# Splitting the final RMSNorm over the output projection, and reordering loads around the merge loop, in a one-layer hybrid decoder kernel

## The reference, cut to what matters

```python
merged = sigmoid(gate_r) * (ret_branch @ w_ret_proj) + sigmoid(gate_s) * (sb_branch @ w_sb_proj)
h = x + merged @ w_out
r = lax.rsqrt(jnp.mean(h * h, axis=-1, keepdims=True) + EPS_RMS)
y = h * r * final_norm_gain                  # y_prompt (512 x 2048), y_sample (64 x 2048)
```

## Time and profile before

| | |
|---|---|
| three timed runs | 2132.35, 2132.97 (median), 2134.16 us |
| profiled execution, its own time | 2128.34 us |
| its span, first to last instruction | 2126.6 us |
| mean granted TensorE clock | 0.988 |
| PE, DVE, ACT, POOL busy | 97%, 70%, 45%, 6% |

### The profile page before, as it was taken

One profiled execution on the slowest core, in us unless ns is written; L12 is line 12 of the kernel. 1 busy time (PEld: TensorE's weight loads), 2 busy tenths in 40 slices (PEclk: granted clock), 3 DMA queues, 4 the chain that ended last, 5 costly groups with the idle time before them and its releaser, 6 DMA issues.

```text
span 2126.6 us, 42199 instructions
## 1 busy us (share of the span) xinstructions
PE 2067.3 (97%) x15584; PEld 1989.3 (94%) x15584; DVE 1487.0 (70%) x1915; ACT 965.1 (45%) x1345; POOL 132.7 (6%) x141
## 2 busy tenths in 40 slices
PE   7999999999999999999999999999999989988996
PEld 6999999999999999999999999999999989988996
DVE  6866766666772377778878878878787644457776
ACT  5545545445563345454454444454555521233333
POOL 0022212122200000000000000000000000000000
PEclk9999999999999999999999999999999999999998
DMA  4445554454554443334333343334436353453444
GB/s 152 126 134 145 147 146 141 137 146 139 146 159 141 140 134 114 111 91 120 110 112 113 114 122 113 114 115 121 120 116 211 105 166 116 135 154 102 112 124 140
DMA packets 454611, 276.71 MB, mean 130 GB/s; under 512 B 20595, under 2 KB 434547, under 8 KB 453235
## 3 DMA queue, kind: packets, MB, share of 16 engines
q1 hardware_dynamic: 452340, 270.71, 43.2%
q10 hardware_dynamic: 2176, 4.72, 0.6%
HBM read 235.25 MB, written 40.11 MB: 129 GB/s over the span
## 4 chain that ended last, share of the span: by engine, by line
PE 87%; DVE 6%; DMA 3%; DVEq 2%; ACT 1%; issue 1%; SPq 1%; ACTq 0%
PE ACC L742 42%; PE ACC L748 21%; PE ACC L651 9%; PE Z L671 4%; DMA RAW<-in_w_ret_proj 2%; PE Z L796 1%; PE Z L973 1%; PE Z L881 1%; DVE LO L1699 1%; PE Z L855 1%; PE Z L778 1%; PE Z L809 1%; PE Z L982 1%; PE Z L1048 1%; PE Z L957 1%
## 5 line engine op out<-in xcount | busy, mean ns | idle before, releaser
L1241 ACT ACTIVATE HI<-RAW 128x1024 fp32r<-128x1024 f32 x434 | 448.8, 1054 | 603.1 <-PE ACC L748 300.2
L1737 DVE TENSOR_TENSOR LO<-RAW,HI 128x1024 fp32r<-128x1024 f32 x434 | 533.9, 1239 | 199.2 <-ACT HI L1241 167.9
L742 PE MATMUL ACC<-XH,HI 128*128 128x288 f32 x1728 | 471.5, 298 | 0.0
L742 PE MATMUL ACC<-XL,HI 128*128 128x288 f32 x1728 | 464.3, 295 | 0.0
L742 PE MATMUL ACC<-TH,HI 128*128 128x288 f32 x1296 | 360.1, 303 | 0.0
L742 PE MATMUL ACC<-TL,HI 128*128 128x288 f32 x1296 | 353.0, 297 | 0.0
L742 PEld LDWEIGHTS ACC<-XH,HI 128*128 128x128 f32 x1728 | 324.6, 188 | 14.4 <-issue 13.6
L742 PEld LDWEIGHTS ACC<-XL,HI 128*128 128x128 f32 x1728 | 324.4, 188 | 0.2
L748 PE MATMUL ACC<-XH,LO 128*128 128x288 f32 x1728 | 264.0, 294 | 0.0
L742 PEld LDWEIGHTS ACC<-TH,HI 128*128 128x128 f32 x1296 | 243.8, 188 | 3.3 <-ACT HI L1241 1.2
L742 PEld LDWEIGHTS ACC<-TL,HI 128*128 128x128 f32 x1296 | 243.8, 188 | 0.2
(11 more groups left out here) (331 smaller groups left out, 3093.6 us busy)
## 6 DMA issues: line engine op xcount, KB each, us to landing
RAW<-in_w_in SPq DMA_DIRECT2D x224, 512.0 KB, 3.9
KV<-in_cache_sb_k SPq DMA_DIRECT2D x256, 64.0 KB, 1.9
KV<-in_cache_sb_v SPq DMA_DIRECT2D x256, 64.0 KB, 1.9
RAW<-in_w_ret_proj SPq DMA_DIRECT2D x32, 512.0 KB, 4.2
RAW<-in_w_out SPq DMA_DIRECT2D x32, 512.0 KB, 4.4
RAW<-in_w_sb_proj SPq DMA_DIRECT2D x16, 512.0 KB, 3.9
ST<-in_state_ret SPq DMA_DIRECT2D x64, 128.0 KB, 2.7
out<-ST SPq DMA_DIRECT2D x64, 128.0 KB, 3.4
```

The lines of the kernel that those rows point to most:

```text
L742: mm = pe.matmul(to, HI[:, w, k, :], x[:, k, :], start=k == 0 and x is xh, stop=False)
L1241: act.activation(HI[:, SLOT[pos]], RAW[:, SRC[n]], ACT.Copy).then_inc(S["hi_made"], 1)
L1737: dve.tensor_tensor(LO[:, SLOT[pos]], RAW[:, SRC[n]], HI[:, SLOT[pos]].bitcast(F32), ALU.subtract)\
```

## The change

Four things are done.

1. *SP's order.* `merge_in(0, 0)` goes ahead of the fourth weight load (for that the scratch of the gate's logarithm moves from `RT` to the new `GT`). In the loop all four weight loads of a turn are issued before the two `merge_in`. Three blocks of `w_out` (512 KB each) are loaded before the loop.
2. *The joint of the two stages.* `lo(0)`, `sums` and `hi(0)` of the first pair run behind turn 0 of the merge loop. The product of the gate parts becomes `gated_part`, ahead of the wait for the matmuls. `t_low(3)` moves into the first pair, `hi(3)` and `lo(3)` ahead of it.
3. *The norm.* For each pair of output columns (256 wide) ScalarE sums squares (`squares`) and VectorE multiplies by the gain (`weigh`), once a pair later, with a 128 KB broadcast load of the gain per pair (`final_weight`). At the end the partial sums are added (`sum_of`), one scale per row is made (`scales`), and VectorE (blocks 0, 2, 4) and ScalarE (1, 3) multiply by it (`scaled`).
4. *The last pair.* Its last product goes to bank 0 and waits for the third sum instead of the sixth; the sum `Y10` goes ahead of `lo(6)`.

```diff
-        HH, at = sb("HH", [P, 5, D_MODEL], at=ws)
-        YA, at = sb("YA", [P, 2, T], at=at)
+        YA, at = sb("YA", [P, 2, T], at=ws)
         YB, at = sb("YB", [P, 2, T], at=at)
+        HH, at = sb("HH", [P, 5, D_MODEL], at=at)
...
-        FG, _ = sb("FG", [P, D_MODEL], at=raw_at)
-        JF, _ = sb("JF", [P, D_MODEL], at=x_at)
+        GT, _ = sb("GT", [P, 2, T], at=t_at + 50688)
+        F2, at = sb("F2", [P, 2, 2 * P], at=r_at + KT * T * 4)
+        SQ, at = sb("SQ", [P, 5, 8], at=at)
...
             weights(w_ret[0], 8 * P, 0)
+            sp.wait_ge(S["g_out0"], 16 * 8)
+            merge_in(0, 0)
             weights(w_ret[0], 8 * P, 1)
             gates_out(d_gr, 14, RG, 1)
-            sp.wait_ge(S["g_out0"], 16 * 8)
-            merge_in(0, 0)
             sp.wait_ge(S["g_out1"], 16 * 8)
             merge_in(8, 1)
+            block_of(w_out[0], 0, 0, 2, "a11_in")
+            block_of(w_out[0], P, 0, 3, "a21_in")
+            block_of(w_out[0], P, 1, 4, "a22_early")
             with sp.Fori(1, 8) as i:
                 t.enter(i, 1, PER_C)
                 for k in range(2):
                     weights(w_ret[0], (i + 8 * k) * P, 0)
                     weights(w_ret[0], (i + 8 * k) * P, 1)
+                for k in range(2):
                     t.take("mg_used")
                     merge_in(i + 8 * k, k)
                 t.leave(7)
...
-            first_blocks(w_out[0], 0, P)
+            t.reach("raw_free0")
+            block_of(w_out[0], P, 1, 0, "a22_in")
+            t.reach("raw_free1")
+            block_of(w_out[0], 0, 1, 1, "a12_in")
+            def final_weight(k):
+                if k >= 2:
+                    sp.wait_ge(S["weighed"], k - 1)
+                src = final_gain[2 * k * P:2 * (k + 1) * P].rearrange("(o n) -> o n", o=1).broadcast_to([P, 2 * P])
+                sp.dma_start(F2[:, k % 2, :], src).then_inc(S[f"fg_in{k % 2}"], 16)
...
                 lower_blocks(w_out[0], 2 * k * P, (2 * k + 1) * P)
+                final_weight(k - 1)
             residual(KT - 2)
             residual(KT - 1)
-            t.past("lo_made", 5)
-            sp.dma_start(FG[:], final_gain.rearrange("(o n) -> o n", o=1).broadcast_to([P, D_MODEL]))\
-                .then_inc(S["fg_in"], 16)
-            for n in range(4):
-                sp.wait_ge(S["y_done"], n + 1)
+            final_weight(7)
+            for n in (1, 0, 2, 3):
+                sp.wait_ge(S[("y_done", "y_act")[n % 2]], n // 2 + 1)
                 sp.dma_start(y_prompt[0, n * P:(n + 1) * P, :], HH[:, n, :]).then_inc(S["y_out"], 16)
-            sp.wait_ge(S["y_done"], 5)
+            sp.wait_ge(S["y_done"], 3)
...
             for pos, n in enumerate(LAST):
                 xh, xl = OPER_M[n]
-                to, w = BANK[INTO[n]], SLOT[pos]
+                to, w = BANK[0 if pos == 6 else INTO[n]], SLOT[pos]
...
                 if pos == 6:
-                    t.past("comb", 6)
+                    t.past("comb", 3)
...
                     if first and p == 0:
-                        log_one_plus(RT, RG)
+                        log_one_plus(GT, RG)
...
             merge_body(0, True, False)
+            hi(0, True)
             with act.Fori(1, 7) as i:
                 t.enter(i, 1, PER_C)
                 merge_body(i, False, False)
                 t.leave(6)
             merge_body(7, False, True)
-            hi(0, True)
...
             t_high(2, 7, 8, 31)
+            hi(3)
+            late_high(7)
             t_high(3, 0, 8, 32)
-            late_high(7)
+            def squares(k, lo_, hi_, spare):
+                for n in range(lo_, hi_):
+                    rows = P if n < 4 else NS
+                    if n == 4:
+                        act.drain()
+                    act.activation(spare[0:rows, n % 4 // 2, n % 2 * 2 * P:(n % 2 + 1) * 2 * P], HH[0:rows, n, 2 * k * P:2 * (k + 1) * P], ACT.Square,
+                                   accum_out=SQ[0:rows, n, k:k + 1])
+                act.drain().then_inc(S["sq_done"], 1)
+            def scales(lo_, hi_):
+                t.take("sq_sum")
+                act.activation(RSTD[:, lo_:hi_], SSQ[:, lo_:hi_], ACT.Ln, scale=1.0 / D_MODEL, bias=EPS_RMS)
+                act.drain()
+                act.activation(RSTD[:, lo_:hi_], RSTD[:, lo_:hi_], ACT.Exp, scale=-0.5)
+                act.drain().then_inc(S["rs_f"], 1)
+            def scaled(n):
+                act.activation(HH[:, n, :], HH[:, n, :], ACT.Copy, scale=RSTD[:, n:n + 1]).then_inc(S["y_act"], 1)
             for p in range(7):
                 def after(n):
-                    pass
+                    if p and n == 5:
+                        t.take("h_sum", 2)
+                        squares(p - 1, 0, 5, (YB, YA)[p % 2])
                 def ready():
                     if p == 0:
-                        act.wait_ge(S["lows_made"], 23)
-                pair((YA, YB)[p % 2], ready, after, p == 0, 3 if p == 0 else 0)
-            def square(n):
-                rows = P if n < 4 else NS
-                act.activation(JF[0:rows, :], HH[0:rows, n, :], ACT.Square, accum_out=SSQ[0:rows, n:n + 1])
-                act.drain()
-                act.activation(RSTD[0:rows, n:n + 1], SSQ[0:rows, n:n + 1], ACT.Ln, scale=1.0 / D_MODEL,
-                               bias=EPS_RMS)
-                act.drain()
-                act.activation(RSTD[0:rows, n:n + 1], RSTD[0:rows, n:n + 1], ACT.Exp, scale=-0.5)\
-                    .then_inc(S["rs_f"], 1)
+                        act.wait_ge(S["mg_used"], KT)
+                pair((YA, YB)[p % 2], ready, after, p == 0, 4 if p == 0 else 0)
             for pos, n in enumerate(LAST):
                 hi(n, False, pos)
                 if pos == 2:
                     t.past("prod", 1)
                     act.activation(YB[:, 0, 0:HALF], BANK[0], ACT.Copy).then_inc(S["p1_copied"], 1)
+                if pos == 4:
+                    t.take("h_sum", 2)
+                    squares(6, 0, 5, YA)
             act.wait_ge(S["rows_done"], 1)
-            square(0)
-            square(1)
+            squares(7, 0, 2, YA)
+            scales(0, 2)
+            act.wait_ge(S["weighed"], 8)
+            scaled(1)
             act.wait_ge(S["rows_done"], 2)
-            for n in range(2, 5):
-                square(n)
+            squares(7, 2, 5, YA)
+            scales(2, 5)
+            act.wait_ge(S["weighed"], 9)
+            scaled(3)
...
-            def sums():
+            def sums(early=False):
                 t.take("a11_in", 16)
                 t.take("a21_in", 16)
                 dve.tensor_tensor(RAW[:, 3], RAW[:, 2], RAW[:, 3], ALU.subtract)
                 dve.drain().then_inc(S["sum_made"], 1)
-                t.take("a22_in", 16)
-                dve.tensor_tensor(RAW[:, 4], RAW[:, 0], RAW[:, 3], ALU.subtract)
+                if early:
+                    dve.wait_ge(S["a22_early"], 16)
+                    t.skip("a22_in", 16)
+                else:
+                    t.take("a22_in", 16)
+                dve.tensor_tensor(RAW[:, 4], RAW[:, 4 if early else 0], RAW[:, 3], ALU.subtract)
                 dve.drain().then_inc(S["sum_made"], 1)
                 dve.tensor_tensor(RAW[:, 2], RAW[:, 4], RAW[:, 2], ALU.add).then_inc(S["sum_made"], 1)
...
                 t.take("a12_in", 16)
                 dve.tensor_tensor(RAW[:, 4], RAW[:, 1], RAW[:, 4], ALU.subtract).then_inc(S["sum_made"], 1)
                 after(2)
-                lo(3)
+                if made < 4:
+                    lo(3)
...
+            def gated_part(s):
                 t.take(f"mg_in{s}", 48)
                 dve.tensor_tensor(MGI[:, s, 1, :], MGI[:, s, 1, :], MGI[:, s, 2, :], ALU.mult)
+            def merged_tile(s):
                 t.take(f"acc_dve{s}")
                 dve.tensor_tensor(two(MGI[:, s, 0, :]), acc(s), two(MGI[:, s, 0, :]), ALU.mult)
                 dve.drain().then_inc(S[f"acc_read{s}"], 1)
...
                     split()
                     split()
                     if first and p == 1:
-                        argument(RG, RT, RG)
+                        argument(RG, GT, RG)
                     if p == 1:
+                        gated_part(0)
                         merged_tile(0)
                         early_low(i)
                     if p == 3:
+                        gated_part(1)
                         merged_tile(1)
                         for j in (2, 0, 1, 3):
                             operand(j, i)
                         late_low(i)
             merge_body(0, True)
+            lo(0)
+            sums(True)
             with dve.Fori(1, 7) as i:
                 t.enter(i, 1, PER_C)
                 merge_body(i, False)
...
             for p in range(2):
                 split()
                 split()
+            gated_part(0)
             merged_tile(0)
             early_low(7)
             split()
-            lo(0)
-            sums()
+            gated_part(1)
             for j in range(3):
```

(67 more changed lines are left out.)

## The result

| | before | after |
|---|---|---|
| median of four timed runs, us | 2132.73 | 2105.33 |
| lowest, highest | 2132.35, 2134.16 | 2104.28, 2106.68 |
| profiled execution, its span | 2128.34, 2126.6 | 2104.28, 2102.5 |
| mean granted TensorE clock | 0.988 | 0.993 |

The ratio is 0.987, with a 95% interval of 0.985 to 0.989: 27.4 us faster, at 2105.33 us, where 2105 was forecast. The two profiled executions are only 24.1 us apart. In a second comparison (e9) the same pair of kernels gave 2127.82 and 2106.14, which is 21.7 us faster, a ratio of 0.990 (0.988 to 0.991).

A forecast was written before the change was run, and what follows sets the result against it. TensorE, 87% of the chain of waits, was taken to bound the kernel. Gains of 13.4 + 10.2 + 0 + 4.3 = 27.9 us made the span 2098.7, and with the timed runs' difference 2105 us; range 2098 to 2114.

The forecast's parts named there:

- Merge loop, turns 1 to 7: Merge loop after turn 0: the fifth quarter's stall goes, turns become bound by TensorE at 25.55 us each.
- rival b: Merge loop: late merge_in makes VectorE's splits late, keeping most of the 15.3 us of stalls; 2118 us, chance 0.09.
- Turn 0: First merge turn: new 5.5 us stall at quarter 8 replaces the old; first product 13.4 us earlier, including later turns.
- the prediction's own sign of being wrong: Turn 0 or the pairs: the forecast is wrong if new waits there add up to 10 us.
- The joint: From first product to second pair: the 6.34 us stall and half clock go, one 1.1 us stall stays; gain 10.2 us.
- The pairs: The seven pairs after the joint: weigh and squares fit into gaps, with 0.4 us left for weigh; gain nothing.
- Rival (d): Pairs: squares cost 2.1 us each, making hi(6) late and halving the clock; 45 us, 2150 us, chance 0.02.
- Last pair and tail: End of the kernel: gain 1.8 us up to R and 2.5 after it, together 4.3 us.
- rival (a): Tail: scaled runs at twice the rate, then writes bound it; 1.5 us less, 2103.6 us, chance 0.36.
- R: Tail: the time when rows_back and add_rows after the last sum are done; forecast 2108.2 against 2109.95 before.
- The sum: Whole kernel: gains of 13.4, 10.2, 0 and 4.3 make 27.9 us; profiled span 2126.6 becomes 2098.7.
- To carry the 4.6 over: Whole kernel: the profiled execution's 4.6 us under the timed median was assumed unchanged, giving 2105.1 us.

The follow-up runs named there:

- e9: The changed kernel run once more, unaltered: 2106.14 us, 0.990 of the kernel before.
- e2: The changed kernel with SP's old loop order, merge_in between the weight loads: 2116.87 us.
- e11: The kernel before with SP's new loop order and nothing else: 2114.83 us, 0.994 of the kernel before.
- e3: The changed kernel with lo(0), sums, hi(0) of the first pair and the w_out loads back at the joint: 2104.12 us.
- e4: The changed kernel with a second multiplication of weigh's size on VectorE in each of the first six pairs: 2115.16 us.
- e10: The changed kernel with turn 0's loads and sums reordered, and the first pair's weight loads ahead of its residual loads: 2092.34 us.
- e8: The changed kernel with the sample rows (block 4) scaled and written before blocks 2 and 3: 2108.73 us.
- e6: The changed kernel with squares of the first six pairs done four times over: 2129.38 us.
- e7: The changed kernel with VectorE's scaled reading a second tensor as operand: 2107.14 us.
- e1: The changed kernel with the three w_out blocks loaded right after merge_in(0, 0): 2099.85 us.

## Why the prediction was right, point by point

- **Merge loop, turns 1 to 7.** Right: no wait of L666 after turn 0, the load issued ahead of `merge_in`, 1248 matmuls in 166.67 us, 0.1335 us each. e2 and e11 show that the order alone does it. VectorE does wait for `merge_in`, once in each of turns 1 to 7, 11.0 us in all and 2.5 at most (rival b's mechanism), and TensorE doesn't feel it.
- **Turn 0.** Right in kind: a new stall at quarter 8 with half clock after it, from the loads in the queue. Mis-sized: it was put at 5.5 us (4 to 7 in the signs to look for) and is 8.18, and 9.68 in e9; quarter 8 starts at 1713.3, not 1710.9. The landing was reckoned at 328 to 408 GB/s; from 1702 to 1712 us the queue moved 286 to 311, and the third block held SP 2.84 us. It landed at 1711.9, inside the bounds of 1707 to 1713. In e9 a wait of 0.62 us at quarter 11 comes to the 9.68, 10.3 together: the prediction's own sign of being wrong (new waits that add up to 10 us) was just reached there. The new stall more than ate what the early `merge_in(0, 0)` gave. Gain of the merge stretch 10.5 us by the first products' starts, forecast 13.4.
- **The joint.** Right: three stalls of 0.3 to 0.4 us instead of one of 1.1, 24.2 us, gain 9.5 us against 10.2. e3 ties 6.7 of it to the sums.
- **The pairs.** Nothing, as forecast, within 0.5 us, and thin cover: e4 puts it at 0.2 to 0.5 us. The first step between pairs is 0.5 us longer (24.02 against 23.54), as VectorE waits 2.04 us for a block of `w_out`. In e10, with that block ahead of the residual loads, it is 23.53; but in e8, with the order of the changed kernel, it is 23.54 too (a wait of 1.59), so that the order does it is not shown. `squares` cost 2.3 us for five, not 3. Rival (d)'s mechanism exists (e6), at four times the work: at 1.9 us per square (9.4 us for the twenty that stand for five) that kernel is level with the one before, where the prediction put the turn to slower at 1.7.
- **Last pair and tail.** Gain 4.6 us against 4.3: 2.1 up to the last sum (1.8 forecast) and 2.5 behind it, as forecast, but the 2.5 is made of two errors that cancel, so hitting it was luck. `scaled` runs at 1.29 us where the sum took 2.28 from the nearest row: the rule of the Trainium skill's "VectorE: DVE Perf Modes", section "Mode 2×_2P — use both read ports for one tensor" (an fp32 `tensor_scalar` in SBUF gives two results per cycle), is borne out here (1.29 us against 2.35 with two tensors in e7). So rival (a)'s rule holds, and its price of 1.5 us too. But the end came at R + 14.1 (R is 2088.4) all the same, not at R + 12.7: the rival priced the writes at 408 GB/s throughout, and the last 2 us of them run at 172 and 90. The splitting of the norm, which stands first in the title, is worth about these 2.5 us; no run has it alone.
- **A row that was overlooked.** The prediction says that the trace before has no VectorE operation with one tensor from SBUF to SBUF. It has some. Beside L2107 of the earlier trace rows, with two tensors, stands a copy of the same shape with one (a `CAST`, as its output is `fp32r`), and a narrower one:
```profile
L2103 DVE CAST RVS<-RVN 64x256 fp32r<-64x256 f32 x8 | 2.3, 286 | 0.1
L2102 DVE CAST KSB<-KS 64x128 fp32r<-64x128 f32 x8 | 1.8, 222 | 0.1
```
That is 286 ns against 410, and 64 ns for 128 more columns, which makes an estimated 1.2 us at 2048 columns. With these rows rival (a) would have been the better forecast for `scaled`.
- **The sum.** By traces the gain is 24.1 us where 27.9 was forecast, 2.9 of the difference in turn 0. The median was hit to 0.3 us because it fell by 27.4: the timed runs of the kernel before lay 4.4 us above its profiled execution (4.6 by the three that the prediction had), those of the changed one 1.0. To carry the 4.6 over as a constant was a step without a ground, so the exact hit is luck. In the second comparison the medians fall by 21.7 us, from 2127.82: the same gain of 27.9 would have given 2099.9 there, 6.2 us below the 2106.14 measured.

## What to carry to other kernels

In a queue that issues in order, look for a load that needs nothing standing behind one that waits: one added line gave 13 us here (e11). Before moving loads to an "empty" place, add up what is then ahead of the next urgent load; the same three blocks cost 4 to 6 us in one place (the changed kernel against e1), and 20 us earlier the urgent quarter waits no longer for them than without them (3.81 in e1, 3.90 in e3). Work hidden in the gap of a chain is free up to the gap, here 1.9 us, and past it each microsecond is paid in every pair (e4), and it can make the next chain wait as well (e6).

## What the runs showed of the hardware

- Half clock does not follow from a stall's length alone: after 2.71 us it came in the kernel before, after 2.78 in e2 it did not (normal pace from 1895.22), and in e6 four stalls of 2.28 us were without it and the last two of the same size with it.
- The stall of turn 0 was 8.2 to 10.3 us in nine profiled executions with the same loads in turn 0. The changed kernel's own trace is the shortest; e2 has 8.9, the other seven 9.7 to 10.3. Most of the difference arises ahead of the queue of blocks: counted from the start of the merge stretch, the last gates' write is issued after 11.0 us (e2: 11.2) and in the seven after 12.2 to 12.8, and in e9 the weight load that it hangs on takes 5.1 us instead of 3.9.
- Where the 64 sample rows of 8 KB are written, the data rate falls from over 400 GB/s to between 90 and 303 for 2 to 3 us, at the end of the changed kernel and in the middle of the writes in e8. In the kernel before, the last two full microseconds run at 139 and 131, behind about 390.
